# Shift and scale of the first norm from fp32 blocks of the adaLN matrix, modulation and two projections taken feature block by feature block

## What is computed

```
ada = silu(c) @ w_ada + b_ada                 # c: one vector for the prompt, one for the sample
sh1, sc1, gt1, sh2, sc2, gt2 = split(ada, 6)  # 1024 columns each
h = rms_norm(x, g_pre_mix) * (1 + sc1) + sh1
z = h @ w_in                                  # queries, keys, values, indexer, gates
...                                           # sparse attention, differential attention, gates, SwiGLU
```

## Time and profile before

| | |
|---|---|
| median of 3 runs | 1123.53 us (1122.75 to 1128.28) |
| the profiled execution, its own time | 1120.27 us |
| its span in the profile | 1118.5 us |
| TensorE busy | 996.6 us, 89% of the span |
| mean granted clock | 0.954 |
| VectorE, ScalarE, GpSimd busy | 485.4, 438.7, 469.0 us |
| first projection's first matmul | 62.90 us after the start |

### The profile page before, as it was taken

One profiled execution on the slowest core, in us unless ns is written; L12 is line 12 of the kernel. 1 busy time (PEld: TensorE's weight loads), 2 busy tenths in 40 slices (PEclk: granted clock), 3 DMA queues, 4 the chain that ended last, 5 costly groups with the idle time before them and its releaser, 6 DMA issues.

```text
span 1118.5 us, 17476 instructions
## 1 busy us (share of the span) xinstructions
PE 996.6 (89%) x6944; PEld 953.7 (85%) x6944; DVE 485.4 (43%) x791; ACT 438.7 (39%) x738; POOL 469.0 (42%) x260
## 2 busy tenths in 40 slices
PE   3768998999998999858899848999999999999995
PEld 1468888999998989858789727999999999999995
DVE  4957796777765233156654374222222222100005
ACT  4446323465566544354465323222222222222220
POOL 4686104554454231113447646334343343343440
PEclk9679999999999999989999966999999999999998
DMA  8433102132321111056655400222222221222212
GB/s 301 170 105 125 43 7 100 64 106 93 120 82 60 39 49 60 22 188 229 213 177 220 179 19 19 93 77 75 92 76 80 89 75 42 100 96 84 79 53 84
DMA packets 33660, 111.54 MB, mean 100 GB/s; under 512 B 4224, under 2 KB 7296, under 8 KB 33216
## 3 DMA queue, kind: packets, MB, share of 16 engines
q1 hardware_dynamic: 30080, 102.75, 27.0%
q10 hardware_dynamic: 3248, 6.65, 1.6%
q0 software_dynamic: 272, 1.31, 0.3%
HBM read 100.38 MB, written 10.32 MB: 99 GB/s over the span
## 4 chain that ended last, share of the span: by engine, by line
PE 67%; issue 9%; DVE 5%; ACT 3%; POOL 3%; DMA 2%; SPq 0%; ACTq 0%; DVEq 0%; POOLq 0%
PE pj L1532 45%; PE pj L1730 11%; PE pvb L1641 3%; DMA rawa<-in_w_ada 2%; PE lg L1504 2%; PE tb L1625 2%; PE pj L1703 1%; PE lg L1753 1%; PE lg L1755 1%; PE lg L1754 1%; POOL hf L1023 1%; ACT ahi L877 1%; PE pj L1523 1%; DVE ymix L1419 0%; POOL ro L1056 0%
## 5 line engine op out<-in xcount | busy, mean ns | idle before, releaser
L1532 PE MATMUL pj<-hh,whi 128*128 128x288 f32 x1248 | 279.3, 306 | 21.9 <-DVE hl L1203 21.9
L1532 PE MATMUL pj<-hh,wlo 128*128 128x288 f32 x1248 | 270.8, 299 | 0.0
L1532 PE MATMUL pj<-hl,whi 128*128 128x288 f32 x1248 | 270.2, 299 | 0.0
L1532 PEld LDWEIGHTS pj<-hh,whi 128*128 128x128 f32 x1248 | 203.2, 192 | 25.7 <-DVE hl L1203 14.5
L1532 PEld LDWEIGHTS pj<-hl,whi 128*128 128x128 f32 x1248 | 204.3, 192 | 0.0
L1532 PEld LDWEIGHTS pj<-hh,wlo 128*128 128x128 f32 x1248 | 204.1, 192 | 0.0
L1004 POOL TENSOR_TENSOR wlo<-raw,whi 128x1024 fp32r<-128x1024 f32 x53 | 130.8, 2468 | 111.2 <-ACT whi L708 100.7
L1123 POOL TENSOR_TENSOR wlo<-raw,whi 128x1024 fp32r<-128x1024 f32 x41 | 97.9, 2388 | 165.7 <-ACT whi L971 165.7
L1450 DVE TENSOR_TENSOR ft<-pj,sg 128x576 f32<-128x576 f32 x22 | 16.7, 758 | 193.3 <-PE pj L1532 193.3
L1138 POOL TENSOR_TENSOR dlo<-rawd,dhi 128x1408 fp32r<-128x1408 f32 x16 | 51.6, 3223 | 82.7 <-ACT dhi L954 82.7
L708 ACT ACTIVATE whi<-raw 128x1024 fp32r<-128x1024 f32 x69 | 72.2, 1052 | 31.5 <-PE lg L1504 18.6
(11 more groups left out here) (190 smaller groups left out, 1922.4 us busy)
## 6 DMA issues: line engine op xcount, KB each, us to landing
raw<-in_w_s SPq DMA_DIRECT2D x94, 512.0 KB, 3.5
rawa<-in_w_ada SPq DMA_DIRECT2D x32, 512.0 KB, 3.8
rawd<-in_w_d SPq DMA_DIRECT2D x16, 704.0 KB, 4.1
raw<-in_w_ada SPq DMA_DIRECT2D x16, 512.0 KB, 5.1
g_raw<-gz ACTq DMA_DIRECT2D x16, 288.0 KB, 2.1
gate<-g_raw SPq DMA_DIRECT2D x8, 576.0 KB, 3.8
rawv<-in_w_v SPq DMA_DIRECT2D x8, 324.0 KB, 4.8
xt<-in_xT SPq DMA_DIRECT2D x2, 1152.0 KB, 6.5
```

The lines of the kernel that those rows point to most:

```text
L1532: ins = mm(pj[tile % 2][:, h, 0:HALF], w[:, slot(c), b:b + P], x[:, kc, h * HALF:(h + 1) * HALF], start=(kc == first and w is whi and x is ...
```

## The change

The first 2048 columns of `w_ada` are laid out on the host as 16 blocks (`w_blk`): block `2*kc` is the scale of feature block `kc`, block `2*kc+1` its shift, each 1024 rows by 128 columns, again 512 KB. Such a block is now the stationary operand, in plain fp32, and the two conditioning vectors move: 8 matmuls of 2 columns a block (`ada_block`). The result stands at once with features on the partitions, in one of four PSUM places. VectorE adds the bias (`take_block`) and makes `gs` of that feature block. No splitting of these chunks remains on ScalarE or VectorE, no copy of rows, no transposes. The sum of squares and the product with `rstd0` go from GpSimd to VectorE, the modulation from GpSimd to ScalarE (two ACTIVATE with scale and bias for each feature block). The small constants are loaded before the first block, `xt` after the fourth. The last eight blocks are interleaved with the first two projection chunks (`N_FIRST = 2`), feature block by feature block.

```diff
-            for c in range(N_ADA0 + 3):
-                load(c)
-                if c == 1:
-                    for dst, src in ((ident, "ident"), (bada, "bada"), ...
+            for b in range(N_BLK):
+                if b >= RAW0:
+                    sp.wait_ge(blk_full, b - RAW0 + 1)
+                sp.dma_start(raw0[:, b % RAW0, :], a["w_blk"][b]).then_inc(raw0_in[b % RAW0], 16)
+                if b == 3:
+                    for h in range(2):
+                        sp.dma_start(xt[:, 4 * h:4 * h + 4, :], a["xT"][:, 4 * h:4 * h + 4, :]).then_inc(x_in[h], 16)
+                if b in (7, 9):
+                    load((b - 7) // 2)
...
+            rms(tile_of["stat0"], rms0, 0)
             for kc in range(KC):
+                act.wait_ge(gs_ready, kc + 1)
+                act.wait_ge(xn_ready, kc + 1)
+                if kc >= 3:
+                    act.wait_ge(h_lo, kc - 2)
+                for w, c0, c1 in SPANS:
+                    ins = act.activation(hf0[:, kc % 3, c0:c1], xt[:, kc, c0:c1], ACT.Identity,
+                                         bias=ada[:, kc, w:w + 1], scale=gs[:, 0, kc, w:w + 1])
+                ins.then_inc(hf_ready, 1)
...
+            def take_block(b):
+
+                kc, shift = divmod(b, 2)
+                col = kc if shift else KC + kc
+                v.wait_ge(blk_full, b + 1)
+                v.tensor_tensor(ada[:, col, :], ada_bank(b), bada[:, col, :], ALU.add).then_inc(blk_read, 1)
+                if shift:
+                    v.wait_ge(blk_read, b)
+                    v.tensor_scalar(gs[:, 0, kc, :], ada[:, KC + kc, :], 1.0, gains[:, 0, kc:kc + 1], ALU.add, ALU.mult)\
+                     .then_inc(gs_ready, 1)
...
+            for b in range(4):
+                take_block(b)
+            v.wait_ge(sq_ready, 2)
+            v.tensor_tensor(acc0[:, :], sq0[:, 0, :], sq0[:, 1, :], ALU.add).then_inc(acc_ready, 1)
...
+            v.reciprocal(rstd0[:, :], rms0[:, :]).then_inc(rstd_ready, 1)
+            v.wait_ge(rstd_ready, 1)
+            normalise(0)
+            normalise(1)
+            for b in range(4, 8):
+                take_block(b)
...
             for kc in range(KC):
+                if kc + 2 < KC:
+                    normalise(kc + 2)
+                take_block(N_BLK - KC + kc)
                 modulated_lo(0, hf0[:, kc % 3, :], hh, hl, kc)
...
+            def ada_block(b):
+
+                pe.wait_ge(raw0_in[b % RAW0], 16 * (b // RAW0 + 1))
+                if b >= 4:
+                    pe.wait_ge(blk_read, b - 3)
+                for kc in range(KC):
+                    ins = mm(ada_bank(b), raw0[:, b % RAW0, kc * P:(kc + 1) * P], cf[:, kc, :], start=(kc == 0),
+                             stop=(kc == KC - 1))
+                ins.then_inc(blk_full, 1)
...
+            for b in range(4):
+                ada_block(b)
+            stat(tile_of["stat0"], [acc0], [(acc_ready, KC - 1)])
+            for b in range(4, N_BLK - KC):
+                ada_block(b)
...
+            for kc in range(KC):
+                ada_block(N_BLK - KC + kc)
+                pe.wait_ge(h_lo, kc + 1)
+                for c in range(N_FIRST):
+                    if kc == 0:
+                        wait_lo(pe, c)
+                    ins = blocks(c, tile_of[c], [kc], hh, hl, 0, KC - 1)
+                    if kc == KC - 1:
+                        ins.then_inc(pj_full, 1)
```

More of the change, by code:

```diff
@@ L88, in plan @@
 def plan():
-    ch = [("ada", n, q) for n in range(4) for q in range(4)]
-    ch += [("ki", 0)] + [("qi", j) for j in range(4)]
+    ch = [("ki", 0)] + [("qi", j) for j in range(4)]
     ch += [("kb", 0), ("qb", 0), ("kb", 1)]
@@ L122, in project @@
     def project(c, waiting, values=()):
-        s.extend([("part", AT[c], 0, KC)] + [("split", w) for w in waiting] + [("end", AT[c])]
+        s.extend([("part", AT[c], 0, KC)] * (AT[c] >= N_FIRST) + [("split", w) for w in waiting] + [("end", AT[c])]
                  + [("vsplit", k) for k in values])
@@ L381, in build @@
         rawa_in = [sem(f"rawa_in{i}") for i in range(RAW_A)]
-        x_in = sem("x_in")
+        x_in = [sem(f"x_in{i}") for i in range(2)]
         a_hi, a_lo = sem("a_hi"), sem("a_lo")
@@ L736, in rms @@
                    .then_inc(pj_act, 1)
[L738 to L744, removed]
-            for kc in range(KC):
+            rms(tile_of["stat0"], rms0, 0)
+            for kc in range(KC):
+                act.wait_ge(gs_ready, kc + 1)
[6 more added lines that the diff above has]
+                ins.then_inc(hf_ready, 1)
                 act.wait_ge(hf_ready, kc + 1)
                 act.activation(hh[:, kc, :], hf0[:, kc % 3, :], ACT.Copy).then_inc(h_hi, 1)
-                if kc in (1, 3):
-                    hi(N_ADA0 + 1 + kc // 2)
+                if kc in (0, 1, 5):
+                    hi(kc - kc // 5 * 3)
             act.wait_ge(lam_dots, 1)
@@ L1025, in modulate @@
                 ins.then_inc(hf_ready, 1)
[L1027 to L1033, removed]
+            for c in range(RING):
+                lo(c)
             pool.wait_ge(trig_in, 32)
@@ L1181, in _, with normalise @@
             v.tensor_reduce(lam[:, 0:2], lamv[:, 0:2, :], AX.X, ALU.add).then_inc(lam_dots, 1)
[L1182 to L1191, removed]
+            def take_block(b):
[7 more added lines that the diff above has]
+                     .then_inc(gs_ready, 1)
+            def normalise(kc):
+                v.tensor_tensor(xt[:, kc, :], xt[:, kc, :], rstd0[:, :], ALU.mult).then_inc(xn_ready, 1)
+            for b in range(4):
+                take_block(b)
+            v.wait_ge(sq_ready, 2)
+            v.tensor_tensor(acc0[:, :], sq0[:, 0, :], sq0[:, 1, :], ALU.add).then_inc(acc_ready, 1)
+            for kc in range(2, KC):
+                v.wait_ge(sq_ready, kc + 1)
+                v.wait_ge(acc_ready, kc - 1)
+                v.tensor_tensor(acc0[:, :], acc0[:, :], sq0[:, kc, :], ALU.add).then_inc(acc_ready, 1)
+            v.wait_ge(pj_act, taken(tile_of["stat0"], "A"))
+            v.reciprocal(rstd0[:, :], rms0[:, :]).then_inc(rstd_ready, 1)
[4 more added lines that the diff above has]
+                take_block(b)
             def gain_scale(n, sc):
@@ L1535, in blocks @@
                 return ins
[L1537 to L1546 removed]
+            pe.wait_ge(consts, 2)
+            pe.wait_ge(c_silu, 1)
+            for b in range(4):
[4 more added lines that the diff above has]
+            for c in range(N_FIRST):
+                pj_free(pe, tile_of[c])
+            for kc in range(KC):
+                ada_block(N_BLK - KC + kc)
+                pe.wait_ge(h_lo, kc + 1)
+                for c in range(N_FIRST):
+                    if kc == 0:
[3 more added lines that the diff above has]
+                        ins.then_inc(pj_full, 1)
+            pe.wait_ge(misc_in, 16 * 5)
+            pe.wait_ge(c_lo, 1)
             def outputs(src, dst):
@@ L1562, in _ @@
             sets = 0
-            pe.wait_ge(h_lo, 1)
             for s in SCHED:
@@ L1570, in _ @@
                     for kc in range(k0, k1):
-                        if c == N_ADA0:
-                            pe.wait_ge(h_lo, kc + 1)
                         ins = blocks(c, tile_of[c], [kc], hh, hl, 0, KC - 1)
@@ L1810 @@
     w_ada = _np.stack([chunk(x["w_ada"][0][q * 256:(q + 1) * 256, n * 512:(n + 1) * 512])
-                       for n in range(12) for q in range(4)])
+                       for n in range(ADA0, 12) for q in range(4)])
+    w_blk = _np.stack([chunk(x["w_ada"][0][:, i * P:(i + 1) * P]) for kc in range(KC) for i in (KC + kc, kc)])
     tokens = _np.concatenate([x["x_sample"][0], x["x_prompt"][0]], axis=0)
```

152 lines of the change are left out of this document (51 added, 101 removed).

## The result

The change made the kernel slower: 1137.02 us (median; 1135.84 to 1145.11) against 1123.72 us, a ratio of 1.0126, 95% interval 1.0072 to 1.018. The profiled execution took 1137.14 us, its span 1135.0 us, 16.5 more than before. The forecast was 1143.

A forecast was written before the change was run, and what follows sets the result against it. The head was taken as bound by engines other than TensorE. Its steps summed to the eighth `hl` at 97.4 against 75.4 us, +22 on 1120.3, 1142, said as 1143 us for the median; range 1114 to 1152, the forecast's own 1134 to 1152.

The forecast's parts named there:

- 1. first block: Start of the head: constants issued first, the first adaLN block issued near 4 us and landing near 7 us.
- 2. four blocks, low clock: Head, ahead of the norm: four fp32 blocks at the low clock take 14.3 us, ending at 21.3 us.
- 3. seven adds, behind the blocks: VectorE takes the blocks first, so its seven adds start at 21.4 us, 0.76 us each, ending at 27.2 us.
- 4. `stat0`: Ones sum on TensorE behind the adds: four passes of 288 columns, low 0.48 us each, ending at 29.4 us.
- 5. norm, hidden; blocks 4 to 7: Root, reciprocal, products end at 35.6 us, hidden under blocks 4 to 7: 12.9 us at clock 0.56, to 42.5 us.
- 6. steps; eighth `hl`: Interleaved loop: eight steps of 7.2 us, TensorE's 5.65 us of it at clock 0.6; eighth `hl` at 97.4 us.
- part behind the head: From the eighth `hl` to the last value-weight split: 33.4 us of transfers, ScalarE and VectorE, taken as unchanged.
- the upper bound: Price of an fp32 pass in a block, taken from above: 0.112 us at the high clock, 0.22 at half.
- The early query chunk: Second projection done early puts TensorE about 6.4 us ahead behind the head; costed at nothing.
- the clock column: Sign in the profile after: PEclk of 0.6 in the first 100 us; above 0.9 if the clock stays high.
- The loads are cheap at the low clock: Rival for the head's blocks: 0.11 us a pass at low clock, -1 us, 1119 to 1123 us; chance 0.17.
- The clock stays high: Rival for the head: 2.4 GHz through the loads, steps of 4.95 us, -6 us, 1114 to 1117; chance 0.31.

The follow-up runs named there:

- e2: The changed kernel with N_FIRST = 1, only the key chunk projected feature block by feature block, the first query chunk behind it: 1141.56 us, ratio 1.0136.
- e5: The changed kernel measured once more, nothing altered: 1147.76 us, ratio 1.0216.
- e9: e8 with N_FIRST = 1, only the key chunk interleaved and the first query chunk projected behind it: 1103.02 us, ratio 0.9839.
- e8: e6's order with 128 moving columns a pass, and ScalarE's root taken ahead of the first two high parts: 1109.55 us, ratio 0.9892.
- e10: The changed kernel with 128 moving columns a pass and each `hl` made ahead of taking the next block, only these two edits: 1118.05 us, ratio 0.9957.
- e4: The kernel before the change, with only the adaLN matrix's two parts kept as separate tensors: 1119.83 us.
- e6: The changed kernel, still 2 moving columns, reordered: `hl` first, TensorE one block further ahead, adds behind two blocks, two high parts before the root: 1123.75 us, ratio 0.998.
- e3: The changed kernel with VectorE making `hl` before taking the next block's result, last step as it was: 1126.45 us, ratio 1.0049.
- e1: The changed kernel with 128 moving columns a pass in place of 2, the further results unread: 1126.58 us, ratio 1.0044.

## Why the prediction was right, step by step

| step | predicted | first measurement |
|---|---|---|
| 1. first block | near 7 us | 7.62 |
| 2. four blocks, low clock | 21.3 | 21.44 |
| 3. seven adds, behind the blocks | 27.2 | 27.57 |
| 4. `stat0` | 29.4 | 29.9 |
| 5. norm, hidden; blocks 4 to 7 | 35.6; 42.5 | 35.9; 43.4 |
| 6. steps; eighth `hl` | 7.2 us; 97.4 | 6.0 to 7.5, the last 8.8 us; 97.71 |
| part behind the head | 33.4 us | 33.5 |

**What held.** The head moved by 22.3 us where 22.0 was summed, by the steps named: the fp32 block at 3.41 us, the adds late behind it, the norm under blocks 4 to 7. The pace of 0.213 us a pass was taken from the upper bound (0.22). The early query chunk moved TensorE ahead and earned at most 0.8 us up to the first gate: without it `hl` and gate came 8.1 and 8.4 us earlier in e2 (against e5), 4.2 and 3.4 in e9 (against e8).

**What was off.** In step 6 two errors offset each other. The 0.6 was a mean, but the clock has two levels: most steps ran wholly low (3.41 + 2.9 + 1.0, near 7.4 us), three of 6.0 to 6.6 us had some passes high. And the last step's own chain, block, gain, `hf`, `hh`, `hl`, with 3.07 us of TensorE's wait, was not in the sum. Step 5's 0.56 is such a mean too: 12.9 us were summed for blocks 4 to 7, and at the low level they took 14.2. In e5 fewer passes were high, and the eighth `hl` came at 99.48 us. Of the signs, the clock column did not turn out as said, 0.6 in the first 100 us: it reads 1.00 up to 61 us, also where all rows are low, so that its 0.69 for the steps is too high as well. The forecast's own range is uneven: 1152 has the 3.2 us of the median in it, 1134 hasn't.

**What was not in it.** The part behind the head was held to be unchanged. It lost 3.4 us before the feed-forward part (every kernel with the new head: 481.0 to 485.5 us from the first gate to the first `ft`; with the old one 478.8 to 479.2). Where it shows first is ScalarE, after the change and then before:

```profile
532.97 1.06 ACT L872 ACTIVATE ahi<-rawa 128x1024 fp32r<-128x1024 f32 x1 [5.55 <-DMA rawa<-in_w_ada]
```

```profile
507.79 1.06 ACT L877 ACTIVATE ahi<-rawa 128x1024 fp32r<-128x1024 f32 x1 [3.24 <-DMA rawa<-in_w_ada]
```

All ten traces with the new head have a wait of ScalarE for such a chunk of over 5 us (5.12 to 6.06), the three with the old head none above 4.44. In front of this one SyncE's queue stands 1 us longer at a chunk's issue:

```profile
524.72 1.42 SPq L588 DMA_DIRECT2D raw<-in_w_s  x1
```

```profile
501.85 0.43 SPq L598 DMA_DIRECT2D raw<-in_w_s  x1
```

That issue is not the cause by itself: the kernel before has one of 1.46 us at 553.59 us without such a wait, and e10 has the wait (5.13 us) without the issue. Layout was excluded by e4, and the kernels with another order in the head (e6 to e10) have the longer stretch too; what it is stays open. The 9.8 us of the feed-forward part went the other way in the first measurement alone. So the +16.5 us of the profiled span are +22.9 at the first gate (22.3 of it at the eighth `hl`), +3.4 and -9.8. That 1137 lies close to 1143 owes something to luck, since the last two terms were in no sum; the better estimate of what the change does is e5's +25 us. The forecast's own range, 1134 to 1152, holds both measurements.

**The rivals.** *The loads are cheap at the low clock* is refuted: a pass took 0.213 us there and, with the clock up, (1.89 - 0.19) / 15 = 0.113 us (0.19 us is the last load's own row). Both prices taken from above, 0.112 and 0.22, were close. The rule of the Trainium skill (page "TensorE: Matmul & The Clock Gate", section "LDWEIGHTS (loading the stationary operand)"), columns over 1.2 GHz, gives an estimate of 107 ns for 128 columns, which these traces come near at the high clock only. *The clock stays high* was wrong for this order, yet e3 (without the waits) and e1 (with the width) show that blocks as such don't keep it low; its step of 4.95 us is e1's 4.6.

That the low clock costs the change its time is shown by e1 (width alone: 21 us under e5, and the blocks' rows nearly halved) and e3 (waits alone: 21 us). What the clock wants is not settled. With two columns it fell in e6 behind a wait of 0.47 us and held in e3 through one of 0.39 us (both by the weight loads' rows), and in the change itself it rose between two waits of 1 us, at 58 to 61 us, and fell again. With 128 columns it held in e1 through 1.24 us a step and once 1.84, and fell in the steps only once, behind 2.31 and 1.39 us in one step.

## What to carry to other kernels

fp32 matmuls with few moving columns are priced by their weight loads, two for each matmul, and by the clock at which these run; price such a stretch at either level and not at a mean. Where an engine's clock can fall, a wait of 1 us a step may cost three times its length (e3: 6.5 us of waits, 21 us of time; with the clock held up, e10, it cost its own length): put the operation that TensorE waits for ahead of those that only follow TensorE (e3), and see what a queue holds ahead of the one operation on the chain (e8). Follow the same events through both traces down to the end before a difference of 1% is put down to the change: here 9.8 us of it was the run.

## What was not expected of the hardware

- In the trace of the change the clock column reads 1.00 up to 61 us, while up to 58 us every pass takes nearly twice the time that it has at the high level (0.213 us against 0.113). Durations of rows are the safer sign.
- Feed-forward matmuls ran at 129 ns in the first profiled execution of the change (310 in 40 us) and at 132 to 132.5 ns (302 or 303) in the twelve others.
- Passes that move 128 columns took 1.8 us a block (e1) and passes that move two took 3.4: doing 64 times the work was faster, for the clock it got. With the clock up, two columns took 1.8 us as well (e3).
